# Expert rows of all four token tiles fetched by one 8 KB request per row, with sums four rows behind the dot and no rows ahead of the tick

## What is computed

```python
idx = e1 * PEER_NKEYS + e2                    # 8 heads x 16 experts per token
gate = jax.nn.softmax(best, axis=-1)
...
act = jax.nn.gelu(jnp.einsum('phkd,pd->phk', u_tab[ib], tb)) * gb
return jnp.einsum('phk,phkd->pd', act, v_tab[ib])
...
return rmsnorm_2(x, norm_final_w)             # after x + peer_ffn(...)
```

## Time and profile before

| | |
|---|---|
| median of 3 runs | 3864.22 us |
| profiled execution | 3893.29 us |
| its span (first to last instruction) | 3891.2 us |
| busy: PE | 3402.1 us, 87% |
| busy: DVE | 1984.3 us, 51% |
| busy: ACT | 939.9 us, 24% |
| busy: POOL | 1109.7 us, 29% |
| moved by DMA | 1076.49 MB |

### The profile page before, as it was taken

How to read it: one execution, slowest core, us unless ns; L and a number is a source line. 1 busy time by engine, 2 the same in 40 slices (tenths; PEclk the granted TensorE clock), 3 DMA queues, 4 the chain that set the end, 5 groups by cost and what they waited for, 6 DMA issues and landing times.

```text
span 3891.2 us, 47383 instructions
## 1 busy us (share of the span) xinstructions
PE 3402.1 (87%) x17847; PEld 2214.1 (57%) x17847; DVE 1984.3 (51%) x4549; ACT 939.9 (24%) x2133; POOL 1109.7 (29%) x1281
## 2 busy tenths in 40 slices
PE   7999999999999999899989999998677897655555
PEld 4566545555555578788878887765455544111111
DVE  3341263733222388211363257787778436676764
ACT  4452043200000222110342221125423222212212
POOL 1000003352233100000000136654647663333432
PEclk9999999999999999999999999999788999777877
DMA  4439985997884333699322369998869999999998
GB/s 181 152 131 325 327 266 145 311 312 226 255 244 152 139 127 123 221 384 326 114 87 85 125 260 408 412 393 309 304 238 381 412 380 395 421 421 392 421 421 341
DMA packets 337277, 1076.49 MB, mean 277 GB/s; under 512 B 22728, under 2 KB 101013, under 8 KB 292149
## 3 DMA queue, kind: packets, MB, share of 16 engines
q1 hardware_dynamic: 222688, 508.04, 38.2%
q0 software_dynamic: 113968, 565.16, 36.9%
q10 hardware_dynamic: 420, 0.62, 0.1%
HBM read 1045.43 MB, written 236.98 MB: 330 GB/s over the span
## 4 chain that ended last, share of the span: by engine, by line
PE 66%; DVE 14%; DMA 10%; ACT 5%; issue 4%; POOL 1%; another core or an unknown queue 1%; SPq 0%; DVEq 0%; ACTq 0%; POOLq 0%
PE bank L1005 23%; PE bank L3270 9%; PE bank L3496 5%; DMA arena<-expert_rows,arena 4%; DMA ring<-expert_rows,arena 4%; PE bank L3237 4%; DVE ring L2769 3%; PE bank L3003 3%; PE bank L3069 2%; PE bank L3200 1%; DVE arena L2769 1%; PE bank L745 1%; DVE arena L2663 1%; PE bank L2995 1%; PE bank L2973 1%
## 5 line engine op out<-in xcount | busy, mean ns | idle before, releaser
L3496 PE MATMUL bank<-arena 64*64 64x512 f32 x2520 | 398.9, 702 | 147.0 <-ACT arena L2044 120.6
L1005 PE MATMUL bank<-hT,ring 128*128 128x256 f32 (+1 forms) x1536 | 443.7, 451 | 2.1 <-ACT hT L888 1.7
L1005 PE MATMUL bank<-arena,ring 128*128 128x256 f32 (+1 forms) x1536 | 442.1, 450 | 0.0
L1005 PEld LDWEIGHTS bank<-hT,ring 128*128 128x128 f32 x1536 | 291.1, 190 | 153.4 <-issue 120.2
L1005 PEld LDWEIGHTS bank<-arena,ring 128*128 128x128 f32 x1536 | 291.8, 190 | 148.9 <-issue 121.5
L3270 PE MATMUL bank<-hT,ring 128*128 128x256 f32 x1536 | 361.3, 393 | 16.5 <-DVE hT L2485 10.2
L3496 PE MATMUL bank<-ring,arena 64*64 64x512 f32 x1256 | 240.7, 783 | 134.5 <-ACT arena L2044 131.3
L3270 PEld LDWEIGHTS bank<-hT,ring 128*128 128x128 f32 x1536 | 297.1, 197 | 83.0 <-issue 35.2
L1521 POOL DMA_INDIRECT ring<-in_peer_u,arena x256 | 281.8, 1101 | 214.6 <-DVE ring L2769 98.5
L2769 DVE SCALAR_TENSOR_TENSOR ring<-ring,xT 128x1024 f32<-128x1024 f32 x256 | 309.4, 1221 | 31.6 <-DMA ring<-in_peer_u,arena 29.9
L1563 POOL DMA_INDIRECT arena<-in_peer_v,arena x240 | 270.9, 1129 | 176.5 <-issue 57.8
(11 more groups left out here) (609 smaller groups left out, 5346.4 us busy)
## 6 DMA issues: line engine op xcount, KB each, us to landing
expert_rows<-in_peer_u SPq DMA_DIRECT2D x32, 2048.0 KB, 19.9
expert_rows<-in_peer_v SPq DMA_DIRECT2D x32, 2048.0 KB, 21.8
ring<-in_mlp_w SPq DMA_DIRECT2D x32, 2048.0 KB, 11.4
ring<-in_ada_w SPq DMA_DIRECT2D x24, 2048.0 KB, 10.5
late_weights<-in_mlp_w SPq DMA_DIRECT2D x32, 1024.0 KB, 14.6
ring<-late_weights SPq DMA_DIRECT2D x32, 1024.0 KB
ring<-weights_kept SPq DMA_DIRECT2D x32, 1024.0 KB
s_store<-arena POOLq DMA_DIRECT2D x8, 2816.0 KB, 9.8
```

Source lines behind the costliest of these rows:

```text
L1005: last = pe.matmul(bank[:, 0:hi - lo], w[:, k, m * P:(m + 1) * P], x[:, k, lo:hi], start=(k == 0), stop=(k == 7))
L3496: last = pe.matmul(banks[2 * r + n][QUADS[r if y == 0 else 1 - r], :], diag[QUADS[r], (v + y) % V_SLOTS, :], v_part(v + y)[QUADS[r], 512 * ...
```

## The change

All 512 rows are fetched by `both_tables_row`, one request of 8 KB per token out of `expert_rows`. Rows 0 to 207 use 8 places of 8 KB (the memory of the former 8 u and 8 v places), later rows 11. A request waits until the row that held its place before is summed (or added). `EARLY`, the doubled ticks and the separate v requests are gone: row u has its dot in tick u, gelu and acts go in groups of 2 at ticks u+2, the diagonals at u+3, the sum at u+4. The wait for the copied table moves from row 256 to row 0. Since the choice of a unit is placed by the tick of its first row, the choices of units 4 to 7 move from ticks 98, 123, 142 and 165 to 103, 135, 167 and 199.

```diff
+F_SLOTS, F_WIDE, F_MORE = 8, 208, 11
+def both_slot(u):
+    return u % F_SLOTS if u < F_WIDE else (u - F_WIDE) % F_MORE
+def both_before(u):
+    if u < F_WIDE + F_SLOTS:
+        return u - F_SLOTS
+    return u - F_MORE if u >= F_WIDE + F_MORE else None
...
             def both_tables_row(u):
-                i = u - F_FROM
-                if i == 0:
+                before = both_before(u)
+                if u == 0:
                     pool.wait_ge(S("rows_kept"), F_KEPT)
...
+                elif before >= 0 and added(before):
+                    pool.wait_ge(S("v_added"), rows_added(before + 1))
+                elif before >= 0:
+                    pool.wait_ge(S("v_used"), rows_summed(before + 1))
...
+            for u in range(ROWS):
+                both_tables_row(u)
...
-                for g, w in groups_at(k, AGROUP, 2):
-                    act.wait_ge(S("u_used"), g + w)
-                    act.activation(gelus[:, g % 16:g % 16 + w], dots[:, g % 64:g % 64 + w], ACT.Gelu_apprx_tanh).then_inc(S("gelus_ready"), 1)
+                for g in row_at(k, 2):
+                    if g % 2 == 0:
+                        act.wait_ge(S("u_used"), g + 2)
+                        act.activation(gelus[:, g % 16:g % 16 + 2], dots[:, g % 64:g % 64 + 2], ACT.Gelu_apprx_tanh).then_inc(S("gelus_ready"), 1)
...
-                for u in U_ROWS[k]:
+                for u in row_at(k, 0):
                     row_product(u)
...
                 for step, n in SIDE.get(k, ()):
-                    for u in U_EARLY[step, n]:
-                        row_product(u)
                     side(step, 1, n)
...
             for k in TICKS:
-                for v in rows_at(k, SUM_LAG + 1, F_SUM):
...
+                v = k - F_SUM
+                if 0 < v <= ROWS and v % EXPERTS == 0:
+                    halves_crossed(v // EXPERTS - 1)
+                row_pair(v)
```

More of the change, by code:

```diff
@@ L199, with row_at @@
               "xsum": 1, "xq": 1, "xscore": 1, "xturn": 1, "xout": 1, "wo": 1, "fsum": 1, "pq": 1}
-V_FROM, V_SLOTS = 208, 14
-F_FROM, F_SLOTS = 2 * EXPERTS, 11
+V_SLOTS = 14
 F_ACT, F_DIAG, F_ADD, F_SUM, F_END = 2, 3, 3, 4, 3
[L207 to L229, removed]
-def both_landed(u):
[L234 to L254, removed]
+F_SLOTS, F_WIDE, F_MORE = 8, 208, 11
+def row_at(k, lag):
+    return [k - lag] * (0 <= k - lag < ROWS)
+def both_slot(u):
[4 more added lines that the diff above has]
+    return u - F_MORE if u >= F_WIDE + F_MORE else None
+def both_landed(u):
+    i = both_slot(u)
+    return f"u_landed{i}" if i < ERING else f"v_landed{i - ERING}", 16 * sum(both_slot(x) == i for x in range(u + 1))
 def steps(name, lo, hi):
@@ L373 @@
 DOT_GROUPS = 16
[L374 to L392, removed]
 TILE_END = {"swap": 0, "rows": 2, "scale": 4}
@@ L400, in tile_end @@
     for t in range(2):
[L401 removed]
+        if k == (t + 1) * EXPERTS + F_SUM + (TILE_END[step] + 1 if t else 0):
             return t
@@ L463, in gather_tickets @@
     for k in range(ROWS + TILE_LAG + 1):
-        for v in rows_at(k, SUM_LAG + 1, F_SUM):
-            if v % EXPERTS == 0 and 0 <= v < ROWS:
+        for v in row_at(k, F_SUM):
+            if v % EXPERTS == 0:
                 t.append((f"ffn{v // EXPERTS}", 4, (0, 1, 2, 3)))
@@ L3501, in _ @@
             for k in TICKS:
-                for v in rows_at(k, SUM_LAG + 1, F_SUM):
-                    if v == EXPERTS:
-                        for step, n in SIDE.get(k, ()):
-                            side(step, 1, n)
-                    if 0 < v <= ROWS and v % EXPERTS == 0 and v != F_FROM:
-                        halves_crossed(v // EXPERTS - 1)
-                    row_pair(v)
-                if F_FROM + SUM_LAG + 1 in old_ticks(k):
-                    halves_crossed(F_FROM // EXPERTS - 1)
+                v = k - F_SUM
+                if 0 < v <= ROWS and v % EXPERTS == 0:
+                    halves_crossed(v // EXPERTS - 1)
+                row_pair(v)
                 if k == ADD_FLUSH:
@@ L3516, in _ @@
                     tokens(tokens_at(k))
-                if EXPERTS not in rows_at(k, SUM_LAG + 1, F_SUM):
-                    for step, n in SIDE.get(k, ()):
-                        side(step, 1, n)
+                for step, n in SIDE.get(k, ()):
+                    side(step, 1, n)
 def kernel(**inputs):
```

83 lines of the change are left out of this document (20 added, 63 removed).

## The result

| | us |
|---|---|
| before, median (lowest to highest) | 3862.4 (3859.8 to 3866.1) |
| changed, median (lowest to highest) | 3939.6 (3928.1 to 3944.8) |
| ratio, 95% interval | 1.0195 [1.017, 1.022] |
| forecast | 3902, range 3850 to 3965 |

The change is slower by 77 us; 38 were forecast. The sign, the range and the mechanism at the end of the gather hold; the size is twice the forecast. In a later session the changed kernel gave 3931.1 us (ratio 1.0168 [1.015, 1.0185]), so 66 to 77 us are to be explained. Its profiled execution took 3940.8 us, its span is 3938.7 us.

The account below looks back on a forecast made before the run. Time was taken as the side job up to tick 214, plus the bytes then left over 421 GB/s. Terms 6 - 14 - 3 + 8 + 18 + 23 = +38 us on 3864.2 gave 3902 us, range 3850 to 3965.

Parts of the forecast that it names:

- mechanism at the end of the gather: After tick 214: rows no longer fetched early remain to be moved at the DMA's 421 GB/s, +23 us.
- first stage, to tick 80: Ticks 4 to 80: 6.3 MB more requested, partly offset by faster 8 KB pieces, +6 us.
- work taken off DVE's chain: 2620 to 2950 us: 15 dots and one unit's choice leave DVE, 53% of 27 us counted, -14 us.
- six dots at `xscore`: 2950 to 3132 us: six dots ahead of their tick go, easing waits on u parts, -3 us.
- more gelus: ACT in the side job: 53 more gelus and 21 more table loads, a fifth of 38 us counted, +8 us.
- shorter lags: Ticks 80 to 214: DVE waits for a gelu at 67 even ticks, mostly covered by its dot, +18 us.
- tail: From tick 214's dot to the last dot: 317.2 MB at 421 GB/s plus two tile ends, 766.4 us, +23 us.
- Bounds of the stages: PE and DMA limit ticks 4 to 80, dependent steps 2620 to 2950 us (chain stage), PE to tick 214, then DMA.
- second rival: Side job: DVE waits for the gelu with no cover, 100 us instead of 18, 3984 us; chance 0.12.
- The step from the profile to the median: Difference worked out against the profiled execution of 3893.29 us, then put on the runs' median of 3864.2 us.
- The first: Rival: chain stage and `xscore` shorten by more than the tail pays, -24 us, 3840 us; chance 0.18.
- The third: Rival: side job's relief just pays for the tail's 23 us, no measurable change, 3864 us; chance 0.14.

Follow-up runs that it names:

- second profile of before: The kernel before, unchanged, run and profiled a second time: 3862.6 us, ratio 0.9995, profiled execution 3865.1 us.
- no rows ahead: The kernel before without its 34 rows dotted ahead of their tick, doubled ticks moved from 222 to 250: 3889.0 us, ratio 1.0063.
- gelus of 2: The kernel before with gelus of 2 rows instead of 4 in tiles 0 and 1, all lags kept: 3869.7 us, ratio 1.0014.
- gelu a tick earlier: The changed kernel with ACT's gelu of two rows one tick earlier, behind that tick's diagonals: 3937.7 us, ratio 1.0193.
- gelu and diagonals: The changed kernel with tile 1 ending early, and both the gelu and the diagonals one tick earlier: 3929.0 us, ratio 1.0161.
- the early end: The changed kernel with tile 1's swap, norm rows and scale at the earlier ticks that tiles 2 and 3 have: 3925.9 us, ratio 1.0158.

## Why the prediction was right in sign and half in size

The terms, with what the profiles give (the table; the last dot is 75.2 us later than in the second profile of before, 77 on the medians):

| term | forecast | measured | from |
|---|---|---|---|
| first stage, to tick 80 | +6 | +5 | changed against before |
| work taken off DVE's chain | -14 | -15 | no rows ahead, to tick 168 |
| six dots at `xscore` | -3 | -7 | the same, 168 to 214 |
| more gelus | +8 | +5 | gelus of 2 |
| shorter lags | +18 | +39 to +44 | what is left of ticks 80 to 214 |
| tail | +23 | +40 | changed against before |

- **Bounds of the stages.** Right. What was said of the chain stage (fewer than 291 GB/s, less on the chain through DVE) and of the tail (421 GB/s, two dips) is in the windows. Tick 214's dot is at 3148.7 us, inside 3110 to 3170. DVE's gelu waits, 79 us, lie outside the 10 to 40 that were to speak for the forecast and near the 100 of the second rival; yet that rival's mechanism is not what cost time.
- **First stage, DVE's chain, `xscore`, gelus.** Four terms within 4 us, partly by luck. Each measured entry but that of the gelus compares single profiles, and two profiles of one kernel differ by 15 us (before) and by 4 (changed) between ticks 80 and 214. For DVE's chain, 14 us were 53% of 27; in the run without rows ahead DVE lost 44 (21 dots lay between ticks 99 and 165, not 15, and a unit's choice is some 17 us, not 8, since the rows summed for it leave steps out), so the 15 us measured are a third of it: too little work times too high a share. That POOL is never waited for is misread too, by the 2.8% of the second line of the earlier trace rows; no run shows that this mattered. For the gelus, the drain that the Trainium skill ("ScalarE: Activation LUTs", "What ACT_TABLE_LOAD costs") states would have made the term about +14, as an estimate. By the trace's 1283 ns a load it was +8, and the run gave +4.6 us.
- **Shorter lags: the term that failed, 18 us for a measured 39 to 44.** The prediction priced one link, DVE's wait for the gelu, and put the others at nothing: "PE's pair now needs a diagonal of one tick before instead of two; in the chain stage PE has time", and a row requested four ticks ahead of its dot is "enough". PE's busy share of that stage, 74% before, says nothing of the ticks where PE runs without a gap, as around tick 92, and there it now stops. Each link by itself is indeed cheap in the kernel before: the product at the gelu's tick cost nothing, the diagonal a tick later 3.5 us. Inside the changed kernel, moving a link within the four ticks from dot to sum gave nothing (gelu a tick earlier; gelu and diagonals). One tick more from dot to sum gave 20 us of the side job back; two more, with the same places, cost 34. So what failed is the pricing of each link as if the others kept their slack.

  What the runs point to in its place is a ring: dot, gelu, product, diagonal, pair, request into the place that comes free, dot eight rows on. With less distance between the engines, a stop of one reaches the next sooner. Against the run without rows ahead, the changed kernel's second profile loses 12 us in ticks 82 to 106, 15 in 106 to 130, 9 in 130 to 168 and 6 in 168 to 214. In the second of these stretches PE's stops for diagonals are 23 us against 5.5; with the sum a tick later they are 7, and 6 of the 15 us come back. In the first, DVE used to run ahead: when it is at its dot of tick 98, ACT has last begun a diagonal of tick 94 and PE a pair of tick 93 in the second profile of before, and of ticks 95 and 96 in the changed kernel's. That the ring, and not one part of it, makes the 39 to 44 us is inferred from these runs; no run shows it by itself.
- **Tail: two smaller misses.** The bytes are right to the row (309.2 MB), and the forecast of 766.4 us from tick 214 missed the measured 774.2 by 8. That is about the end of tile 1, which was given the 6.5 us of tile 2's: the early end takes 8 to 9 us off. The other 9 us are on the side of before: 743.4 us in the prediction's profile, 734.4 in the second.
- **The step from the profile to the median.** The prediction took its difference against an execution that stood 29 us over the median and laid it on the median as if the 29 us were in both. The second profile shows 24 of them in the side job and tail. Against the prediction's own profile tick 214 came 16 us later, the +15 of its terms, but only because that execution's side job was 16 us long; against the second profile it came 35 us later, 4 of them before the gather.
- **Rivals.** The first needed 31 us of relief; without rows ahead it was 22. The third needed terms that cancel; the shorter lags took that away.

What stays open: how the 39 to 44 us divide between the short links and the 8 places. Two single links were tried, and longer lags with the same places. Not tried were the request that waits for a sum instead of a dot, by itself (short lags with the two requests of 4 KB would show it), the gelus of 2 with short lags, where their table loads stand ahead of diagonals, and short lags with more places, for which the memory has no room before row 208. The 39 to 44 us are also what is left when other terms are taken off, and hold whatever else the change moved. No version of the runs beats the kernel before; the best of the changed ones, with the early end and the sum a tick later, is still 1.2% slower.

## What to carry to other kernels

When a change shortens several lags at once, write down the ring that they close (who frees the place, who asks for the next row, who waits for it), and look in the trace of before how many ticks each engine is ahead of the next at the busiest places: a lag shorter than that lead can become a stop, even where each link alone is nearly free. Here such a lead shows at a few ticks only, around 90 to 98 and 182 to 186, so it does not account for the whole loss. A stage's busy share doesn't say that an engine has time; look at the ticks where it runs without a gap, and at what stands ahead of the awaited instruction in the other engine's list. And before a difference is laid on a median, see that the profile is an ordinary execution: take a second one if its own time is over the runs.

## What the runs showed that was not expected

- The same program's profiled executions differ by 28 us (3893.3 and 3865.1) at equal DMA bytes, 15 us of it between ticks 80 and 168, the chain of dependent steps, where the DMA share is 0.81 to 0.84. What set the two executions apart is not known.
- Waits of 57 us on DVE, and of 24 us more on PE, that cost 0 and 3.5 us: a total of waits, even on an engine of the chain, is no estimate of a cost.
